# Prompt attention in a two-layer decoder step: turn, values and result of two-map units one step later

## The reference

```python
s = einsum('bqhmd,bkhmd->bmhqk', q, k) * (DC ** -0.5) + bias
s = where(dist >= 0, s, -inf)
p = softmax(s, axis=-1)
return einsum('bhqk,bkhd->bqhd', p[:, 0] - lam * p[:, 1], v)
```

## Time and profile before

| | us |
|---|---|
| median of the runs | 3136.27 |
| lowest run | 3132.68 |
| profiled execution | 3126.44 |
| its span in the trace | 3124.8 |
| PE busy | 2949.7 (94%) |
| DVE busy | 1400.6 (45%) |
| ACT busy | 612.0 (20%) |

### The profile page before, as it was taken

The page is one execution under the profiler, slowest core; times in us unless marked ns, Lnnn a source line. Parts: engine busy times, 40 slices in busy tenths (PEclk is TensorE's granted clock), DMA queues, the critical chain, the costliest instruction groups (busy, mean ns, idle before and its releaser), DMA issues.

```text
span 3124.8 us, 45956 instructions
## 1 busy us (share of the span) xinstructions
PE 2949.7 (94%) x16570; PEld 2403.4 (77%) x16570; DVE 1400.6 (45%) x2838; ACT 612.0 (20%) x1261; POOL 173.2 (6%) x207
## 2 busy tenths in 40 slices
PE   7999999998888899999989999999998879999997
PEld 5888888888765578888868888888886657788885
DVE  5444545216654244445454454450366541544544
ACT  1010002213464311010011000121235542111000
POOL 3000000000032000000000000000002320000000
PEclk8999999999998999999999999999898989999998
DMA  8422122210178632221242212222204685223222
GB/s 164 130 81 81 57 80 69 77 55 31 38 223 242 191 95 81 81 81 52 71 111 81 81 54 85 78 68 67 71 0 148 211 232 156 68 81 84 57 79 66
DMA packets 366170, 301.17 MB, mean 96 GB/s; under 512 B 14738, under 2 KB 338540, under 8 KB 365842
## 3 DMA queue, kind: packets, MB, share of 16 engines
q1 hardware_dynamic: 341756, 217.98, 25.1%
q0 software_dynamic: 24256, 81.11, 8.8%
HBM read 287.21 MB, written 14.45 MB: 97 GB/s over the span
## 4 chain that ended last, share of the span: by engine, by line
PE 87%; DVE 5%; DMA 3%; ACT 2%; issue 2%; DVEq 1%; SPq 0%; POOL 0%; ACTq 0%; POOLq 0%
PE banks L703 25%; PE banks L796 17%; PE banks L853 13%; PE banks L728 5%; PE banks L739 5%; PE banks L667 4%; PE banks L1294 3%; PE banks L972 2%; PE banks L960 2%; PE banks L976 1%; DMA keys_values_by_token<-in_w_gate 1%; PE banks L1125 1%; PE banks L1189 1%; ACT weight_slots L1622 1%; PE banks L873 1%
## 5 line engine op out<-in xcount | busy, mean ns | idle before, releaser
L853 PE MATMUL banks<-normed_or_mixed,weight_slots 128*128 128x272 f32 x1792 | 413.5, 393 | 2.3 <-DVE normed_or_mixed L1776 2.3
L853 PEld LDWEIGHTS banks<-normed_or_mixed,weight_slots 128*128 128x128 f32 x1792 | 340.3, 190 | 73.2 <-DVE normed_or_mixed L1776 3.2
L703 PE MATMUL banks<-normed_or_mixed,arena 128*128 128x272 f32 x1408 | 337.8, 393 | 5.0 <-DVE arena L1828 5.0
L703 PE MATMUL banks<-arena 128*128 128x272 f32 x1408 | 337.0, 392 | 0.0
L703 PEld LDWEIGHTS banks<-normed_or_mixed,arena 128*128 128x128 f32 x1408 | 266.9, 190 | 62.9 <-DVE arena L1828 3.8
L703 PEld LDWEIGHTS banks<-arena 128*128 128x128 f32 x1408 | 267.5, 190 | 55.1
L1372 ACT ACTIVATE hidden_or_projected<-banks 128x1024 f32<-128x1024 f32 (+4 forms) x160 | 137.1, 864 | 222.3 <-PE banks L667 144.9
L796 PE MATMUL banks<-hidden_or_projected,keys_values_by_token 128*128 128x272 f32 x704 | 177.0, 392 | 0.0
L796 PE MATMUL banks<-arena,keys_values_by_token 128*128 128x272 f32 x704 | 169.6, 393 | 1.1 <-DVE arena L1885 1.1
L796 PE MATMUL banks<-hidden_or_projected,weight_slots 128*128 128x272 f32 x704 | 169.2, 392 | 0.0
L796 PEld LDWEIGHTS banks<-arena,keys_values_by_token 128*128 128x128 f32 x704 | 133.4, 190 | 30.0 <-DVE arena L1885 2.8
(11 more groups left out here) (373 smaller groups left out, 4256.1 us busy)
## 6 DMA issues: line engine op xcount, KB each, us to landing
weight_slots<-in_w_down SPq DMA_DIRECT2D x128, 256.0 KB
weight_slots<-in_w_in SPq DMA_DIRECT2D x28, 1024.0 KB
keys_values_by_token<-in_w_gate SPq DMA_DIRECT2D x48, 512.0 KB, 5.1
keys_values_by_token<-in_w_up SPq DMA_DIRECT2D x48, 512.0 KB, 5.2
weight_slots<-in_w_gate SPq DMA_DIRECT2D x40, 512.0 KB, 5.0
weight_slots<-in_w_up SPq DMA_DIRECT2D x40, 512.0 KB, 5.1
hidden_or_projected<-in_cache_win_k SPq DMA_DIRECT2D x112, 128.0 KB, 5.1
weight_slots<-in_w_down SPq DMA_DIRECT2D x64, 192.0 KB
```

Source lines behind the costliest of these rows:

```text
L703: mm = pe.matmul(ps[:, bank, 0:HALF], weights[:, k, :], acts[:, k, :], start=first and k == 0, stop=k == 3, skip_group_check=True)
L853: mm = pe.matmul(half(bank + 2 * u, h), wslot[:, slot, at:at + 128], hT[:, k, h * HALF:(h + 1) * HALF], start=k == 0, stop=k == KD - 1)
```

## The change

For units with two maps (8 to 15) three things move by one step in the programs of their engines. PE: the turn goes from part 0 to part 1 of the next unit and the values from part 1 to part 2. ACT: the copy of the turned weights goes from part 0 to part 1. DVE: the result goes from part 2 of the next unit to part 0 of the one after that, so behind the next unit's weights; that of unit 15 stays in the last step, and so does that of unit 7. Units 0 to 7 keep their steps, and so do scores, logits, maxima, exponentials and weights.

```diff
--- before.py
+++ after.py
@@ -1214,16 +1214,13 @@
 
                 def prompt_step(step):
                     u, part = unit_at(step)
-                    if part == 0:
-                        if u < 16:
-                            prompt_scores(u, 0)
-                        if 0 < u <= 16:
-                            prompt_turn(u - 1)
-                    if part == 1:
-                        if 8 <= u < 16:
-                            prompt_scores(u, 1)
-                        if 0 < u <= 16:
-                            prompt_values(u - 1)
+                    late = 1 if u > 8 else 0
+                    if part < 2 and u < 16 and part < maps(u):
+                        prompt_scores(u, part)
+                    if part == late and u:
+                        prompt_turn(u - 1)
+                    if part == late + 1 and u:
+                        prompt_values(u - 1)
 
                 pe.wait_ge(s["q_sb"], l + 1)
                 pe.wait_ge(s["st_new"], l * 4 + 1)
@@ -1622,7 +1619,7 @@
                                 last = act.activation(row, row, ACT.Exp, bias=p_mx[:, u % 2, 4 + i:5 + i],
                                                       accum_out=p_mx[:, u % 2, 8 + i:9 + i])
                         last.then_inc(s["p_exp"], 1)
-                    if part == 0 and 0 < u <= 16:
+                    if part == (1 if u > 8 else 0) and 0 < u <= 16:
                         n = (u - 1) % 4 + 1
                         act.wait_ge(s["ppt_mm"], l * 16 + u)
                         if u >= 2:
@@ -2298,8 +2295,10 @@
                     u, part = unit_at(step)
                     if part == 0 and 2 <= u <= 8:
                         prompt_result(u - 2)
-                    if part == 2 and 8 <= u <= 16:
+                    if part == 2 and u in (8, 16):
                         prompt_result(u - 1)
+                    if part == 0 and 10 <= u <= 16:
+                        prompt_result(u - 2)
                     if u < 16 and part < maps(u):
                         prompt_logits(u, part)
                         if part == maps(u) - 1:
```

## The result

| | before | after |
|---|---|---|
| median of the runs, us | 3130.28 | 3141.12 |
| lowest run, us | 3124.78 | 3134.97 |
| profiled execution, us | 3126.44 | 3146.19 |
| its span, us | 3124.8 | 3144.5 |

Twelve runs of each give a ratio of 1.0029 (95% interval 1.0017 to 1.0041); one run of before took 5246.4 us, in a slow state, and is left out of the ratio. The 3136.27 and 3132.68 us shown ahead of the prediction are two of these twelve runs, so 3130.28 is the better median of before. The change costs about 9 to 11 us. The forecast was 5.6 us less. The time itself lies in the range given, but the sign is wrong. The profiled execution is among the longest of its runs (3134.97 to 3147.2), so differences between its trace and the trace of before are larger than those between the medians: 19.7 against 10.8 us.

A forecast was written before the change was run, and what follows sets the result against it. TensorE bounds the kernel (87% of the chain), with 37.5 us idle in the stage. Per layer 9.5 - 3.7 - 1.9 - 1.1 = 2.8 us gained, 5.6 in all: 3136.27 - 5.6 = 3130.7 us, range 3118 to 3142.

The forecast's parts named there:

- The clock behind the added wait: Step 37, line 1138: part of the pass at half pace after the wait, 1.9 us a layer, bounds 0 and 3.7.
- The added wait: Step 37: PE waits 3.74 us for unit 12's result, which now stands behind unit 13's weights on DVE.
- The gain up to step 37: Up to step 36: shorter softmax waits, an earlier turn and fewer slow spells win 9.5 us a layer, bounds 3.9 and 9.5.
- The last steps: Step 45: unit 15's values stand behind the last gather, losing 1.1 us a layer; the earlier lead passes through.
- The DMA rival: Late steps: transfers give back all the gain, within 2 us in all, about 3126 profiled; chance 0.24 including the fourth.
- The slower rival: Step 37's wait, clock and last step cost 6.7 us a layer; slower if less is won before; chance 0.14.
- the fourth: Rival: step order changes but PE waits as long, the key copy being always last; chance within the DMA rival's 0.24.
- the third: Rival: clock stays up at step 37 and gathers follow, 15 us less in all; chance 0.12.
- The slower rival's test: Step 37: this rival holds if line 1138 starts later than 991.85 counted from the stage's start.
- Turns and the clock: PE's turns: the skill's transpose rule would make the sum some 3 us a layer worse; the trace, 1.09 and 1.97 us, disagrees.

The follow-up runs named there:

- x7: Changed kernel plus 16 unread products on PE ahead of the second sample-weight pass's wait; ratio to before 0.9998, 3126.81 against 3128.64 us.
- x1: Changed kernel with unit 12's result copied ahead of unit 13's weights again; ratio to before 0.9963, 3120.14 against 3133.3 us.
- x5: Changed kernel with only units up to 12 late and results placed as in before; ratio to before 0.9971, 3119.14 against 3128.64 us.
- x6: Before with only turns and values of units 13 to 15 one step late; ratio to before 1.0014, 3132.96 against 3128.64 us.
- x8: x5 with ACT's first value copy in step 27 ahead of unit 10's exponentials; ratio to before 0.9934, 3107.72 against 3128.64 us.
- x10: x8 with unit 6's result ahead of unit 7's weights; ratio to before 0.9940, 3113.11 against 3128.24 us.
- x2: Before with only unit 12's result moved behind unit 13's weights; ratio to before 1.0068, 3152.45 against 3133.3 us.

## Why the prediction was wrong

**The clock behind the added wait: the step that failed.** The prediction put a slow clock behind the wait of step 37 at 1.9 us, with 3.7 as its upper bound, taking it for a matter of the pass alone. The pass lost 3.4, near the bound, and the steps behind it another 5.5 and 7.2 us in the traces: 9 to 10.6 a layer, and 5 to 6 a layer by the runs' times. x7 shows that it is the clock and not the wait: with the same delay and PE kept busy the loss is gone, 1.0029 against 0.9998. No row of before shows a spell that long: behind unit 12's wait turns are slow at 984.32 and at full pace at 988.72. The fault was to take that length for a bound, and to look no further than the pass.

**What turned the sign.** The forecast was 9.5 - 3.7 - 1.9 - 1.1 = 2.8 us gained a layer. The trace of layer 0 has 6.7 - 3.9 - 8.9 - 2.1 = 8.2 lost. With the clock's 8.9 alone put right the forecast would have been a loss of 4.2; with the 4.9 to 6.3 us of the runs' times it would have been a loss of 0.2 to 1.4, against the 4.6 to 5.4 measured, and most of the rest is the gain that was put too high. With the gain alone put right it would have been 0.0. So the clock is the larger fault, but not the only one.

**The added wait.** 3.74 us forecast, 3.74 found, in both layers, with the releaser named. The order of DVE's program and three rows were enough.

**The gain up to step 37.** Right in its mechanism, too large in its size. The softmax waits went from 9.7 to 0 (under 3 forecast), and line 667 waits 1.7 us for key copies (2 to 4 forecast; 2.9 in x1). I had 8.8 us at the start of step 35 and 9.5 soon after; the trace has 6.7 and 6.8 at step 36, and x1 and x5 5.4 to 5.8. So some 3 to 4 us too much, of which the clock is part. In x1 PE waits 1.89 us for the key copy at 965.90, as forecast, but the slow spell that was to go with the longer wait is still there: 0.50 at 968 to 972. In the changed kernel the clock is low for longer behind the untouched wait in step 28 (2.62 us there, 2.77 in before). Two windows of the changed kernel, then the same of before:

```profile
952.00:956.00 4.00, 4.00 (x33) 2.50 (x33) 0.79 (x1) 1.02 (x1) 0.00 (x0) 0.50 0.54 184
956.00:960.00 4.00, 4.00 (x17) 2.78 (x14) 2.57 (x2) 0.81 (x1) 0.94 (x1) 0.50 0.69 211
```

```profile
952.00:956.00 4.00, 4.00 (x21) 1.93 (x20) 2.83 (x4) 0.00 (x0) 0.94 (x1) 0.65 0.83 218
956.00:960.00 4.00, 4.00 (x49) 2.56 (x47) 0.61 (x1) 1.83 (x2) 0.88 (x1) 0.92 0.63 208
```

**The last steps.** 1.1 us forecast, 2.1 to 2.6 found in x1 and x7, up to 6.3 in layer 1 of x6, none in x5. The DMA rival, which had all of the gain eaten by transfers, is wrong at this size: in x5 and x1 5.4 to 6.3 us pass through to step 38, and in x5 all of it to the end. It holds for leads of some 12 us (x8 in layer 1, x10), where key turns do wait for SP's window keys, as its test said. Waits of line 1159 did grow, from 3.8 to 6.7 us, but in x1 they grew as much (6.8) beside a gain.

**The slower rival** named the right place and the right mechanism and set its point of decision at 6.7 us won before step 37. With 3.9 for the wait, 9 to 10.6 for the clock and 2 for the last steps that point is 15 to 16.6, and still 11 to 12 with the clock's price by the runs' times; the changed kernel had won 6.7. It had 0.14; what argued against it, that units 11 and 12 wait far beyond the key copy, was true and beside the question. The other two rivals fall too: no softmax wait is left (the fourth), and the clock did not stay up at step 37 (the third). The slower rival's test read "line 1138 starts later than 991.85 counted from the stage's start"; it starts 2.8 us earlier, and the loss comes after its start.

**Turns and the clock.** The changed kernel again has turns at 1.09 us (1009.14, clock 0.97) and at 1.97 (995.99, clock 0.50). The Trainium skill (TensorE: Matmul & The Clock Gate, Part 4: PE-mode transpose) says that the full clock doesn't engage for transposes; the sum did come out worse, but not for that reason, and the trace still disagrees.

**What stays open.** Why one spell at the lower clock ends after some 4 us and another after 20. It isn't the length of the wait alone: in the changed kernel 4.60 us of waiting for a gather, at 1020.04, is followed by only about 5 us of it (0.50 at 1020 to 1024, 0.84 at 1024 to 1028). Behind step 28 the spell lasted about 4 us in before and 13 in after, for much the same instructions with one turn moved. And x8 and x10, whose PE programs are the same, wait 2.17 us for a result in step 17 and then turn the same weights and keys, x8 (first two rows) at full pace, x10 at a slower one:

```profile
907.82 0.85 PE L667 MATMUL banks<-constants,weight_slots 128*128 128x128 f32 x6 [2.17 <-DVE normed_or_mixed L2292]
908.50 1.04 PE L667 MATMUL banks<-constants,hidden_or_projected 128*128 128x128 f32 x8
```

```profile
907.39 1.28 PE L667 MATMUL banks<-constants,weight_slots 128*128 128x128 f32 x6 [2.17 <-DVE normed_or_mixed L2292]
908.46 1.91 PE L667 MATMUL banks<-constants,hidden_or_projected 128*128 128x128 f32 x8
```

x6 and x2 lose 1.3 to 1.9 us in step 32 where their programs are those of before (x2 in layer 1 alone). Since such spells differ in length, and since the loss of the last steps that I subtracted (2.1) was 2 to 6 us in other kernels, the 5.5 and 7.2 us are those of one execution; the medians give less.

## What to carry to other kernels

When an instruction is moved behind longer work of the same engine, look for every later wait on its signal, also in code that belongs to something else: here a pass of sample weights counted results of prompt units. Price a wait of several us on TensorE by the clock behind it too, and until when, since that part was 1.3 to 2.8 times the wait here (4.9 to 10.6 us against 3.74); where the wait can't go, products that nobody reads can fill it (x7). A wait that another one covers is no reason to leave either: removed one at a time they gave 0.9971 and 1.0006, together 0.9934.

## What the runs showed of the hardware

The granted clock stayed at 0.50 for about 20 us (988 to 1008; 2528 to 2548 in layer 1) with PE recorded as busy for all or nearly all of it, in products of 64 to 384 columns and transposes, after an idle time of 3.74 us. Shorter waits were also followed by 0.50: 2.62 us in the changed kernel, 1.89 in x1, 2.02 in x8; one of 2.17 us was in x10 (0.62 at 908 to 912) and was not in x8 (1.00). Of the wait's full price of about 10 us a layer (x2), only 3.74 are seen as a wait in the view of waits; the rest appears as busy time and as later gathers. A pass with 3.68 us of other products right before it (x7) kept its 3.78 us.
